# Attention scores in row groups of 64 and 32 partitions, and a new order of VectorE's and GpSimd's work ahead of attention

## The reference, cut to what matters

```python
# MLA, 8 heads, 64 features without rope and 32 with rope; k_rope is one for all heads
q = (rms_norm(c_q) @ w_uq).reshape(B, S, 8, 64 + 32)
q_nope, q_rope = q[..., :64], apply_rope(q[..., 64:], cos, sin)
kv = (rms_norm(c_kv) @ w_ukv).reshape(B, S, 8, 64 + 64)
k_nope, v = kv[..., :64], kv[..., 64:]
k_rope = apply_rope(k_r, cos, sin)
s = (q_nope @ k_nope.T + q_rope @ k_rope.T) * 96 ** -0.5      # per head
o = softmax(s) @ v
# GLA, 4 heads, chunks of 64 tokens, two directions
state = decay * state + k_end.T @ v                            # 7 steps a direction
o_gla = masked(q_dec @ k_inv.T) @ v + q_dec @ state            # then norm, gain, silu gate
# Fourier: real part of an FFT over tokens and channels, then a 64 x 64 product
```

## Time and profile before

| | us |
|---|---|
| median of three runs | 517.47 |
| the profiled execution's own time | 518.39 |
| its span | 516.6 |
| end of the last AV block of attention | 196.01 |
| TensorE busy | 486.3 |
| VectorE busy | 233.1 |
| ScalarE busy | 139.4 |
| GpSimd busy | 75.8 |

### The profile page before, as it was taken

How to read it: one execution, slowest core, us unless ns; L and a number is a source line. 1 busy time by engine, 2 the same in 40 slices (tenths; PEclk the granted TensorE clock), 3 DMA queues, 4 the chain that set the end, 5 groups by cost and what they waited for, 6 DMA issues and landing times.

```text
span 516.6 us, 7659 instructions
## 1 busy us (share of the span) xinstructions
PE 486.3 (94%) x2888; PEld 261.5 (51%) x2888; DVE 233.1 (45%) x579; ACT 139.4 (27%) x363; POOL 75.8 (15%) x101
## 2 busy tenths in 40 slices
PE   4999999899999999999989899999999998989894
PEld 4474444457655554455456455555555553444431
DVE  3499312977757641126763222222222222232166
ACT  4425102355667650222131011111111111112023
POOL 1000000370100000001121222222222222111000
PEclk9999999999999999999999899999999999989998
DMA  8996000010497006931499999999999999999974
GB/s 296 364 271 235 1 1 0 17 37 3 140 419 296 1 1 268 423 122 42 141 320 313 397 390 416 423 417 417 421 417 421 417 417 423 420 419 417 402 288 162
DMA packets 35542, 139.42 MB, mean 270 GB/s; under 512 B 9864, under 2 KB 11976, under 8 KB 23472
## 3 DMA queue, kind: packets, MB, share of 16 engines
q1 hardware_dynamic: 30160, 130.85, 64.8%
q0 software_dynamic: 4816, 7.85, 4.1%
q10 hardware_dynamic: 528, 0.22, 0.2%
HBM read 129.94 MB, written 16.39 MB: 283 GB/s over the span
## 4 chain that ended last, share of the span: by engine, by line
PE 64%; DVE 13%; DMA 13%; SPq 7%; issue 2%; ACT 1%; DVEq 0%; POOLq 0%; ACTq 0%
PE bank L1114 17%; PE bank L976 9%; PE bank L1127 8%; PE bank L815 7%; DMA EW<-in_moe_w_up 5%; PE bank L949 4%; DMA EW<-in_w_in 4%; SPq L644 4%; PE bank L1021 3%; PE bank L1010 3%; PE bank L1086 2%; DMA EW<-y_scratch 2%; SPq L649 2%; PE bank L893 1%; DMA y_scratch<-G,sidx 1%
## 5 line engine op out<-in xcount | busy, mean ns | idle before, releaser
L1114 PE MATMUL bank<-EW,WO 128*64 128x256 f32 x640 | 78.5, 397 | 5.1 <-DMA EW<-in_moe_w_up 2.5
L1114 PEld LDWEIGHTS bank<-EW,WO 128*64 128x64 f32 x640 | 45.0, 137 | 33.2 <-DMA EW<-in_moe_w_up 4.4
L1902 DVE TENSOR_TENSOR G<-G,bank 128x128 f32<-128x128 f32 x32 | 9.2, 288 | 107.2 <-ACT G L1482 105.0
L1482 ACT ACTIVATE G<-bank 128x128 f32<-128x128 f32 x32 | 8.9, 278 | 178.8 <-PE bank L1114 164.6
L976 PE MATMUL bank<-WO,XT 128*128 128x512 f32 x128 | 56.9, 596 | 0.0
L2127 POOL DMA_INDIRECT y_scratch<-G,sidx x30 | 30.8, 1026 | 153.8 <-DVE G L1915 138.4
L1915 DVE COPY G<-bank 128x512 f32<-128x512 f32 x32 | 22.1, 692 | 46.2 <-PE bank L1127 46.2
L1127 PE MATMUL bank<-EW,G 128*64 128x512 f32 x160 | 38.3, 599 | 0.0
L976 PEld LDWEIGHTS bank<-WO,XT 128*128 128x128 f32 x128 | 23.6, 190 | 26.9 <-issue 26.9
L949 PE MATMUL bank<-EW 96*128 96x512 f32 x64 | 32.8, 596 | 0.9 <-ACT WO L1401 0.6
L1767 DVE TENSOR_REDUCE nm<-bank 128x1 f32<-128x512 f32 x32 | 22.0, 689 | 14.3 <-PE bank L949 14.1
(11 more groups left out here) (314 smaller groups left out, 724.7 us busy)
## 6 DMA issues: line engine op xcount, KB each, us to landing
EW<-in_moe_w_down SPq DMA_DIRECT2D x20, 1024.0 KB
EW<-in_moe_w_gate SPq DMA_DIRECT2D x19, 1024.0 KB
EW<-in_moe_w_up SPq DMA_DIRECT2D x19, 1024.0 KB
y_scratch<-MIX SPq DMA_DIRECT2D x8, 512.0 KB, 8.2
WO<-in_w_out SPq DMA_DIRECT2D x2, 2048.0 KB, 12.4
MIX<-in_moe_w_gate SPq DMA_DIRECT2D x4, 1024.0 KB
MIX<-in_moe_w_up SPq DMA_DIRECT2D x4, 1024.0 KB
G<-in_moe_w_down SPq DMA_DIRECT2D x4, 1024.0 KB
```

The costliest lines, as they stand in the source:

```text
L1114: mm = pe.matmul(bank[BLOCK * m:BLOCK * (m + 1), 0:2 * P].rearrange("p (w n) -> p w n", w=2), xeT[:, c, par * BLOCK:(par + 1) * BLOCK], wv ...
```

## The change

- **Layout.** `qT` and `kT` (96 rows a head) go. `qn` and `kn` hold two heads in 128 partitions (64 each) without rope; `qrT` holds, for a pair of heads, four groups of 32 rows (each head's rope part twice), and `krT` the k rope part four times. GpSimd's `rotate` writes its two outputs twice (a broadcast read), into `qr2` and `krp`. Copies out of PSUM are of full width: four instead of eight for kT, qn and the rope part, two an engine. The seven DMAs at L632 go.
- **Scores.** In sets of four (two heads by two token tiles) in banks 0 to 3: two products of 64 rows, four of 32 rows, two of 64 rows, each score being the sum of one of the first or last kind and one of the middle.
- **Order of attention.** Set s, then AV(s - 2), then the four transposes of set s - 1; mixer transposes two in set 3 and two in set 4. PT and mT turn in banks 4 to 6, O has bank 7 alone. Eight probability tiles instead of four. Set 0 comes before fy.
- **Banks ahead of it.** M in 4, the GLA outputs in 0 to 3, the rope transposes (now four) in 4 to 7, AB in 4 to 7, fy in 4 to 7.
- **VectorE.** The folds move behind the V copies; `add_P6(0)` moves ahead of the second direction's sums; only one of its two rope copies stands ahead of the GLA sums, and both spectrum copies come behind the four products.
- **ScalarE.** Its wait for the vg tiles moves from ahead of the ckvT copy to the silu; its rope copies stand one ahead of the squares and one behind.
- **GpSimd.** The rotation of k moves ahead of the two memsets; the one of `att` waits for the first products instead of the vg tiles.

```diff
 def attention_order():
-    for i in range(T * MH + 5):
-        if i < T * MH:
-            steps.append(("S", i))
-        if i == MIX_TURN:
-            steps += [("mT", c) for c in range(4)]
-        if i >= 8 and i % 4 == 0:
-            if i >= T * MH:
-                steps.append(("pre", i // 4 - MH))
-            steps.append(("AV", (i - 8) // 4))
-        if 0 <= i - 3 < T * MH:
-            steps.append(("PT", i - 3))
+    for s in range(SETS + 2):
+        if s < SETS:
+            steps.append(("S", s))
+        if s in MIX_TURNS:
+            steps += [("mT", 2 * MIX_TURNS.index(s) + c) for c in range(2)]
+        if s >= SETS:
+            steps.append(("pre", s - SETS))
+        if s >= 2:
+            steps.append(("AV", s - 2))
+        if 1 <= s <= SETS:
+            steps += [("PT", 4 * s - 4 + j) for j in range(4)]
...
-            def scores(i):
-                ps = open_bank(("S", i))
-                tq, h = attention_item(i)[0:2]
-                close_bank(pe.matmul(ps[:, :], qT[0:QD, h, tq * P:(tq + 1) * P], kT[0:QD, h, :],
-                                     start=True, stop=True), ("S", i))
+            def without_rope(s, tile):
+                for i in range(4 * s + 2 * tile, 4 * s + 2 * tile + 2):
+                    ps = open_bank(("S", i)) if tile == 0 else banks[PLAN[("S", i)][0]]
+                    tq, pair, _, _, u = attention_item(i)
+                    rows = slice(NOPE * u, NOPE * (u + 1))
+                    mm = pe.matmul(ps[:, :], qn[rows, pair, tq * P:(tq + 1) * P], kn[rows, pair, :],
+                                   start=(tile == 0), stop=(tile == 1))
+                    if tile == 1:
+                        close_bank(mm, ("S", i))
+            def with_rope(s):
+                for i in range(4 * s, 4 * s + 4):
+                    tq, pair, _, tile, u = attention_item(i)
+                    ps = open_bank(("S", i)) if tile == 1 else banks[PLAN[("S", i)][0]]
+                    rows = slice(ROPE * (2 * u + tile), ROPE * (2 * u + tile + 1))
+                    mm = pe.matmul(ps[:, :], qrT[rows, pair, tq * P:(tq + 1) * P], krT[rows, :],
+                                   start=(tile == 1), stop=(tile == 0))
+                    if tile == 0:
+                        close_bank(mm, ("S", i))
+            def scores(s):
+                without_rope(s, 0)
+                with_rope(s)
+                without_rope(s, 1)
...
-            for i in range(EARLY):
+            for i in range(T):
                 exponent(i)
                 copy_fy(i)
...
+            for s in range(1, SETS + 1):
+                ahead = 1 if s == 1 else 3
+                for j in range(4):
+                    if s < SETS:
+                        exponent(4 * s + j)
+                    if j == 1 and s in MIX_TURNS:
+                        c = 2 * MIX_TURNS.index(s)
+                        ps = filled(act, ("mT", c))
+                        free_bank(act.activation(xnT[:, c, :], ps[:, :], ACT.Copy), ("mT", c))
+                    if j + 1 >= ahead:
+                        copy_probs(4 * s - 4 + j + 1 - ahead)
+                for j in range(5 - ahead, 4):
+                    copy_probs(4 * s - 4 + j)
...
+            for s in range(SETS):
+                for j in range(4):
+                    row_max(4 * s + j)
+                    if j >= 2:
+                        normalise(4 * s + j - 2)
+                    if j == 2 and s in MIX_TURNS:
+                        c = 2 * MIX_TURNS.index(s) + 1
                         ps = filled(dve, ("mT", c))
                         free_bank(dve.tensor_copy(xnT[:, c, :], ps[:, :]), ("mT", c))
+                for j in range(2, 4):
+                    normalise(4 * s + j)
+                if s >= 3 and s % 2:
+                    copy_heads(s // 2 - 1)
+            copy_heads(MH // 2 - 1)
...
             def rotate(x1, x2, o1, o2, sin, cos, t1, t2, t3, t4):
+                copies = lambda a: a.unsqueeze(2).to_broadcast(list(o1.shape))
...
-                link(pool.tensor_tensor(o1, t1, t2, ALU.subtract))
-                return pool.tensor_tensor(o2, t3, t4, ALU.add)
+                link(pool.tensor_tensor(o1, copies(t1), copies(t2), ALU.subtract))
+                return pool.tensor_tensor(o2, copies(t3), copies(t4), ALU.add)
```

More of the change, by code:

```diff
@@ L102, in psum_plan @@
     for h in range(0, MH, 2):
-        ring(("kT", h), readers=2)
+        ring(("kT", h))
     for c in range(2):
@@ L117, in psum_plan, with middle @@
     for h in range(0, MH, 2):
-        ring(("qn", h), readers=2)
-    use("M", 0)
+        ring(("qn", h))
+    use("M", 4)
     for h in range(GH):
-        use(("o", h), 4 + h)
-    for half in range(2):
-        use(("qrT", half), 1 + half, readers=4)
+        use(("o", h), h)
+    for pair in range(MH // 2):
+        use(("qrT", pair), 4 + pair)
     for i in range(4):
-        use(("AB", i), (0, 3, 1, 2)[i])
-    for i in range(EARLY):
-        use(("S", i), i % 3)
+        use(("AB", i), 4 + i)
+    for j in range(4):
+        use(("S", j), j)
     for t in range(T):
-        use(("fy", t), (3, 4, 5, 7)[t])
+        use(("fy", t), 4 + t)
+    turn[0] = 0
+    def middle(key):
+        use(key, 4 + turn[0] % 3)
+        turn[0] += 1
     for kind, i in attention_order():
-        if kind == "S":
-            if i >= EARLY:
-                use(("S", i), i % 3)
+        if kind == "S" and i:
+            for j in range(4):
+                use(("S", 4 * i + j), j)
         elif kind == "mT":
-            use(("mT", i), (3, 4, 5, 7)[i])
+            middle(("mT", i))
         elif kind == "PT":
-            use(("PT", i), 3 + i % 3)
+            middle(("PT", i))
         elif kind == "AV" and i % 2 == 0:
-            use(("O", i // 2), 6 + i // 2 % 2, fill=0)
+            use(("O", i // 2), 7, fill=0)
     turn[0] = 0
@@ L199, in attention_item @@
     pair, half, tile, u = i // 8, i // 4 % 2, i // 2 % 2, i % 2
-    return 2 * half + tile, 2 * pair + u, i // 4 % 2, tile, u
+    return 2 * half + tile, pair, i // 4 % 2, tile, u
 def shape_constants():
@@ L319, in encoder_kernel @@
         w_in_sb = view(ew01, 0, (C, W_IN))
-        qT = view(ew01, 0, (MH, S))
-        kT = view(ew01, 4096, (MH, S))
+        qn = view(ew01, 0, (MH // 2, S))
+        qrT = view(ew01, 2048, (MH // 2, S))
+        kn = view(ew01, 4096, (MH // 2, S))
+        krT = view(ew01, 6144, (S,))
         V = view(ew01, 8192, (T, MH * MV))
@@ L650, in load_down @@
                              w_down_v[e] if one else w_down_v[e].rearrange("e p n -> p (e n)")).then_inc(dn_landed[place], 16)
-            for half in range(2):
-                drained(sp, ("qrT", half))
+            for pair in range(MH // 2):
+                drained(sp, ("qrT", pair))
             load_gate_up(2, 2)
@@ L934, in _ @@
                             close_bank(mm, ("o", h))
+            for pair in range(2, 4):
+                transpose_rope(pair)
             pe.wait_ge(dft_landed, 16)
@@ L956, in _ @@
                 drained(pe, ("qn", h))
[L957 to L960, removed]
+            for pair in range(MH // 2):
+                drained(pe, ("qrT", pair))
+            scores(0)
             for i in range(4):
@@ L1387, in _, with copy_rope @@
             free_bank(act.activation(fM[:, 2].rearrange("p b n -> p (b n)"), ps[:, 2 * P:], ACT.Copy, scale=-1.0), "M")
[L1388 to L1391, removed]
+            def copy_rope(pair):
+                ps = filled(act, ("qrT", pair))
+                free_bank(act.activation(qrT[:, pair, :], ps[:, :], ACT.Copy), ("qrT", pair))
+            copy_rope(0)
             for h in range(GH):
@@ L1735, in _, with copy_rope @@
                                   gain_gla[:, :].unsqueeze(1).to_broadcast([P, GH, GDV]), ALU.mult).then_inc(gate_ready, 1)
-            for h in range(1, MH, 2):
-                ps = filled(dve, ("qrT", h // 4))
-                rows = slice(ROPE * (h % 4), ROPE * (h % 4 + 1))
-                free_bank(dve.tensor_copy(qT[NOPE:QD, h, :], ps[rows, :]), ("qrT", h // 4))
+            def copy_rope(pair):
+                ps = filled(dve, ("qrT", pair))
+                free_bank(dve.tensor_copy(qrT[:, pair, :], ps[:, :]), ("qrT", pair))
+            copy_rope(1)
             for h in range(GH):
@@ L1760, in _, with copy_heads @@
                                             ALU.mult), ("o", h))
+            copy_spectrum(1)
             copy_spectrum(3)
+            def copy_heads(pair):
+                ps = banks[PLAN[("O", pair)][0]]
+                dve.wait_ge(av_done, 2 * pair + 2)
+                free_bank(dve.tensor_copy(xnT[:, 4 + pair, :], ps[:, :]), ("O", pair))
             def row_max(i):
```

132 lines of the change are left out of this document (54 added, 78 removed).

## The result

The changed kernel takes 512.56 us in the median (512.46 to 512.89, four runs) against 517.58; the ratio is 0.9899, 95% interval 0.9886 to 0.9911. The forecast was 515.2: right in direction, 2.2 times too small a gain. The profiled execution took 512.89, its span 511.1, against 518.39 and 516.6.

A forecast was written before the change was run, and what follows sets the result against it. End of attention gates; TensorE and VectorE alternate ahead of it, then TensorE alone. 1.7 us by fy's end plus 0.6 from cheaper rounds and the earlier fourth score: 2.3 off the 517.47 median gives 515.2, range 510.5 to 519.4.

The forecast's parts named there:

- The round and the passages: Steady attention: overlapped scores save 0.86 us, three more tile-shape passages cost 0.2 each; round falls from 7.3 to 7.05.
- (b): Scores: row groups overlap only in part, the 32-row phase takes 1.12 to 1.17 us; 517.5, no change; chance 0.10.
- (d): Scores: 64-row groups don't overlap at all, the 32-row phase only in part; 529 us; chance 0.04.
- (a): Scores: passages between 64 and 32 rows cost nothing, a set is 0.4 us shorter; 511.0; chance 0.16.
- The hold in set 2: Attention, 133 to 147 us: TensorE's last rope product waits 1.6 to 1.8 us for set 1's fourth exponent.
- (c): Attention: lost look-ahead, late fourth exponents stop TensorE every round, 0.7 us over six rounds; 519.4; chance 0.17.
- 121 to 133 us: Ahead of attention: set 0 starts at 126.2, fy ends at 133.1 instead of 134.78 with one more score done.
- the stretch 89 to 121 us: Ahead of attention: fewer kT copies and later folds let the second L883 start 2.1 us sooner, at 102.0.
- so I look at 89 to 196 us only: Choice of window: the expert stage is unchanged, and no gain was forecast before 89 us.
- After attention: Expert stage: unchanged, so a gain or loss before 196 us goes through to the end one for one.
- GpSimd's doubled outputs: Rotation: writing twice the elements takes 0.7 us an operation, a tile 3.7 instead of 3.2, ending before it is needed.
- (e): Before 104 us: GpSimd's rotations end last and 0.9 to 1.2 of 2.1 us is lost; 516.4; chance 0.07.

The follow-up runs named there:

- e6: Changed kernel with both 64-row score phases first and the 32-row phase last, from set 3 on: 512.65 us.
- e10: Changed kernel with ScalarE doing two exponents, first copy, two exponents, three copies from set 1, and both 64-row phases first from set 3: 510.98 us.
- e1: Changed kernel with GpSimd's old order (two memsets ahead of the rotation of k, both behind the vg tiles): 513.33 us.
- e3: Kernel before with only GpSimd's new order, its scratch tiles moved to a free place: 516.48 us.
- e2: Changed kernel with add_P6(0) put back behind both directions' sums: 517.1 us over twelve runs.
- e11: Changed kernel with ScalarE's wait for the vg tiles ahead of the ckvT copy again: 512.29 us.
- e5: Changed kernel with ScalarE doing three exponents of set 1 before the first copy: 512.37 us.
- e7: Changed kernel with the mixer transposes of sets 3 and 4 behind the AV block: 512.7 us.
- e8: Changed kernel with the edits of e5, e6 and e7 together: 512.54 us.

## Why the prediction was wrong, step by step

- **The round and the passages: right.** 7.05 forecast, 7.06 measured; a set 3.2, measured 3.19; passages 0.2, by e6. Row groups overlap at 512 columns, so rivals (b) and (d) are out; (a) too. Rival (b) has 1.12 us for the 32-row phase without a passage, and it took 1.07 with one. For two groups of 64 rows the full overlap and the passage are shown apart, by e6 and e10; for four of 32 rows only their sum is, and that the split is the same rests on the like phase time and on the overlap of the short products (L877: four start every 0.11 us). The Trainium skill, "TensorEngine Tiling (Array Packing)", Key Properties, says that changing the tiling mode drains the TensorEngine; the traces agree, and the price of 0.2 us is theirs.
- **The hold in set 2: right in place and cause, a little dear.** 1.6 to 1.8 forecast, about 1.2 measured; with the mixer rounds (8.09 for 8.2) this is the 0.6 between 0.6 and 1.2. Rival (c) is out: no later hold.
- **121 to 133 us: right but for 0.2 to 0.4.** From L922 to set 0 it took 6.8 instead of 7.25; the spectrum products 3.5 instead of 3.7.
- **One step that failed: "the stretch 89 to 121 us", 2.1 forecast, 2.6 measured.** It kept the latent scalings at 3.64 and let everything start where it did, "The moved memsets (1.81 and 0.31) lie ahead of the qr copies either way". True for GpSimd's own readers, but what mattered was VectorE beside it. The four scalings, in the trace of before at 0.4 to 1.8 us for the same shape, were the sign: one operation of one shape with a fourfold spread. By e1 the term is 0.79 us in the changed kernel; in the kernel before it is 2.5 us in this stretch, less what the move costs at `add_P6(0)` (e3). The dropped copies and moved folds did what was forecast: without GpSimd's order (e1) it is 12.63 from kT, 2.24 less than before, for 2.1. The Trainium skill, "SBUF — State Buffer", Who interferes with whom, says that a VectorE instruction in a 2-port mode, which `tensor_scalar` can enter, and a GpSimd instruction contend for a shared port pair: the one that issues first has it for its whole length and the other fully blocks. The trace agrees: 1.82 beside a memset of 1.81. By that rule the term could have been in the sum.
- **The other, and the larger: "so I look at 89 to 196 us only", 0 forecast, 0.9 measured.** Two edits lie outside this window or had no term. `add_P6(0)`: 0.85 us in the trace of before (0.58 of waiting and what follows it), more where GpSimd's new order stands without it, up to 4.35 in e2. The vg wait on ScalarE: 0.45 by e11. Together 1.3, less the later start of 0.4 in the traced execution. The first stands in the chain of before (VectorE's L1618 at 49.99 us, with 0.43 of issue ahead of it), the second in its list of waits (ScalarE's L1364 for VectorE's L1618). The rotation of k, moved to 39 to 44 us, had no term there either: in the changed kernel `add_P6(0)` hides it.
- **After attention: right that it passes through one for one**; the marks at 244.71 and 249.21 (L1002, L976) are still 4.5 apart.
- **GpSimd's doubled outputs: right**, 0.73 for the 0.7 taken, and rival (e) didn't come.

In sum: 0.9 from the start, 0.5 from the stretch, 0.2 and 0.6 from the rest are the 2.2 between 2.3 and 4.5. The last 0.5 of the medians' 5.0 lies behind attention and stays open. The direction and the round were forecast for the right reason; that the time lies within the stated range is luck, for the range reached so low for rival (a), which is out.

## What to carry to other kernels

An edit that moves work on one engine can pay on another: ask not only who waits for the moved instruction, but who runs beside it, at the old place and at the new one, and look for an operation of one shape with a wide spread of durations. Before two edits are added up, ask whether one hides the other's cost: GpSimd's move needed `add_P6(0)` moved as well (e2, e3). Cost every line of the diff, and start the window at the first edit, not where the big one is. In a tight handshake removing one wait moves it to the next resource (e5, e7, e8); it took the order of copies and that of products together (e10).

## What the runs showed of the hardware

- A VectorE scaling of 128 x 256 in SBUF takes 0.35 us; beside a GpSimd memset of 1.81 it took 1.82, beside a GpSimd product of 1.03 it took 1.17. A VectorE product of 128 x 1024 takes 1.22 us; beside a GpSimd product it took 1.95.
- TensorE products in different row groups overlap: two of 64 rows and 512 columns take 0.86 plus a passage of 0.2, and two such phases in a row have one passage (1.92). Four of 32 rows take 1.07 with their passage.
- A wait of TensorE of 2.39 us was followed by 3.4 us at half the granted clock (e2), one of 1.61 (e3) was not.
